# The start of a four-layer transformer kernel: x by column halves, its last row blocks turned inside the first weight chunk, and two multiplications of a zeroed tile ahead of them

## The reference

```python
def rms_norm(x, g):
    xf = x.astype(jnp.float32)
    y = xf * lax.rsqrt(jnp.mean(xf * xf, axis=-1, keepdims=True) + NORM_EPS)
    return (y * g.astype(jnp.float32)).astype(x.dtype)
...
h = rms_norm(x, ln1[l])
u = h @ w_in          # 256x1024 times 1024x(about 8000), the first of many such products
```

## Time and profile before

| what | value |
|---|---|
| median of 3 runs | 2510.94 us (2510.31 to 2512.36) |
| span of the profiled execution | 2510.4 us |
| TensorE busy in the span | 2489.0 us (99%) |
| VectorE, ScalarE, GpSimd busy | 1809.0, 1519.6, 154.1 us |
| first transpose of x starts | 6.71 us |
| first multiplication of chunk 0 starts | 10.53 us |
| first multiplication of the narrow product starts | 16.29 us |

### The profile page before, as it was taken

One profiled execution on the slowest core, in us unless ns is written; L12 is line 12 of the kernel. 1 busy time (PEld: TensorE's weight loads), 2 busy tenths in 40 slices (PEclk: granted clock), 3 DMA queues, 4 the chain that ended last, 5 costly groups with the idle time before them and its releaser, 6 DMA issues.

```text
span 2510.4 us, 31997 instructions
## 1 busy us (share of the span) xinstructions
PE 2489.0 (99%) x11868; PEld 2053.5 (82%) x11868; DVE 1809.0 (72%) x1809; ACT 1519.6 (61%) x1581; POOL 154.1 (6%) x133
## 2 busy tenths in 40 slices
PE   8999999999999999999999999999999999999998
PEld 7888888888888888888888887888888888888877
DVE  6587655657775554765555577988989888898888
ACT  6565544555554454545445556777777777777776
POOL 0101000010020000110000023000000000000010
PEclk9999999999999999999999999999999999999999
DMA  6444555444455564555554456999999999999996
GB/s 260 151 159 167 178 186 188 172 160 151 159 177 188 190 207 151 182 181 176 194 185 155 164 193 235 380 370 383 380 382 384 375 384 375 386 373 386 368 406 253
DMA packets 90683, 633.75 MB, mean 252 GB/s; under 512 B 10462, under 2 KB 10838, under 8 KB 15841
## 3 DMA queue, kind: packets, MB, share of 16 engines
q1 hardware_dynamic: 85584, 616.63, 65.7%
q0 software_dynamic: 4720, 15.57, 1.8%
q10 hardware_dynamic: 288, 0.33, 0.0%
HBM read 625.00 MB, written 7.48 MB: 252 GB/s over the span
## 4 chain that ended last, share of the span: by engine, by line
PE 98%; DMA 1%; DVE 0%; issue 0%; ACT 0%; SPq 0%; ACTq 0%; DVEq 0%
PE bank L785 14%; PE bank L787 13%; PE bank L786 13%; PE bank L1360 8%; PE bank L1362 8%; PE bank L1361 8%; PE bank L1333 4%; PE bank L1335 4%; PE bank L1334 4%; PE bank L767 4%; PE bank L800 4%; PE bank L802 4%; PE bank L801 4%; PE bank L1181 1%; PE bank L1180 1%; PE bank L1179 1%
## 5 line engine op out<-in xcount | busy, mean ns | idle before, releaser
L1903 DVE TENSOR_TENSOR w_lo<-raw,w_hi 128x2048 fp32r<-128x2048 f32 x583 | 1342.7, 2305 | 416.7 <-ACT w_hi L1450 401.3
L1450 ACT ACTIVATE w_hi<-raw 128x2048 fp32r<-128x2048 f32 (+1 forms) x588 | 1120.4, 1907 | 264.5 <-PE bank L802 117.4
L785 PE MATMUL bank<-w_hi,xhi 128*128 128x512 f32 x1456 | 580.1, 398 | 0.8 <-DVE w_lo L1913 0.2
L787 PE MATMUL bank<-w_lo,xhi 128*128 128x512 f32 x1456 | 568.7, 391 | 0.0
L786 PE MATMUL bank<-w_hi,xlo 128*128 128x512 f32 x1456 | 568.0, 390 | 0.0
L1360 PE MATMUL bank<-w_hi,xhi 128*128 128x512 f32 x896 | 359.4, 401 | 0.6 <-DVE w_lo L1903 0.3
L1362 PE MATMUL bank<-w_lo,xhi 128*128 128x512 f32 x896 | 350.6, 391 | 0.0
L1361 PE MATMUL bank<-w_hi,xlo 128*128 128x512 f32 x896 | 350.0, 391 | 0.0
L785 PEld LDWEIGHTS bank<-w_hi,xhi 128*128 128x128 f32 x1456 | 273.9, 188 | 61.8 <-issue 4.1
L787 PEld LDWEIGHTS bank<-w_lo,xhi 128*128 128x128 f32 x1456 | 273.5, 188 | 58.3
L786 PEld LDWEIGHTS bank<-w_hi,xlo 128*128 128x128 f32 x1456 | 274.1, 188 | 53.1
(11 more groups left out here) (377 smaller groups left out, 2384.2 us busy)
## 6 DMA issues: line engine op xcount, KB each, us to landing
raw<-in_wexpert SPq DMA_DIRECT2D x336, 1024.0 KB, 5.0
raw<-in_wdense SPq DMA_DIRECT2D x248, 1024.0 KB, 4.7
expert_rows<-y POOLq DMA_DIRECT2D x7, 512.0 KB, 4.8
expert_rows<-back POOLq DMA_DIRECT2D x3, 512.0 KB, 3.9
x<-in_x SPq DMA_DIRECT2D x2, 512.0 KB, 4.5
raw<-in_wdense SPq DMA_DIRECT2D x4, 256.0 KB, 5.9
biasT<-bias_rows POOLq DMA_DIRECT2D x1, 1024.0 KB, 7.1
normal_rows<-hnorm POOLq DMA_DIRECT2D x1, 1024.0 KB, 8.1
```

The lines of the kernel that those rows point to most:

```text
L785: mm(bank[banks[t]][:, :], xhi[:, k0 + k, tok], wh, start=start and k == 0, stop=False)
L787: last = mm(bank[banks[t]][:, :], xhi[:, k0 + k, tok], wl, start=False, stop=stop and k == 3)
L1450: return nc.scalar.activation(dst, src, f, **kw)
L1903: V.tensor_tensor(lo[:, c % RAW, :], raw[:, c % RAW, :], hi[:, c % HI, :].bitcast(F32), ALU.subtract).then_inc(lo_ready, 1)
```

## The change

Three things are done, all in the first microseconds.

1. x comes as two column halves (512 columns of all 256 rows, 512 KB each) in place of two row tiles. The first half has a semaphore of its own, `x_first`. In SyncE's order the first half stands first, then pieces 0 and 1 of chunk 0, then the second half, then pieces 2 and 3; the rest follows as before.
2. TensorE turns only groups 0 and 1 ahead of chunk 0. Groups 2 and 3 are turned in the middle of chunk 0, ahead of its third column block.
3. VectorE first fills 512 columns of `gates` with zeros, and TensorE multiplies this tile with itself twice (float32, 128x512, into bank 7) before it waits for x.

```diff
+            def fetch_piece(i):
+                w = slice(512 * i, 512 * i + 512)
+                sp.dma_start(raw[:, 0, w], a["wdense"][0][:, w]).then_inc(first_in[i] if i < 3 else raw_full[0], 16)
+            def fetch_columns(o, arrived):
+                sp.dma_start(x[:, :, o:o + 512], a["x"][0][:, o:o + 512].rearrange("(t p) d -> p t d", p=P)).then_inc(arrived, 16)
             def fetch_first():
-                for i in range(4):
-                    w = slice(512 * i, 512 * i + 512)
-                    sp.dma_start(raw[:, 0, w], a["wdense"][0][:, w]).then_inc(first_in[i] if i < 3 else raw_full[0], 16)
+                fetch_columns(0, x_first)
+                fetch_piece(0)
+                fetch_piece(1)
+                fetch_columns(512, x_loaded)
+                for i in (2, 3):
+                    fetch_piece(i)
...
-            for t in range(NT):
-                sp.dma_start(x[:, t, :], a["x"][0, t * P:t * P + P, :]).then_inc(x_loaded, 16)
...
                     if ready is None:
-                        pe.wait_ge(x_loaded, 16 * NT)
+                        pe.wait_ge(x_first if i < 2 else x_loaded, 16)
...
                 pe.wait_ge(free[X[1]], ev(key, X[1]))
-                if READY[key] is not None:
-                    norm(key, (2, 3))
+                norm(key, (2, 3))
...
+            pe.wait_ge(warm_set, 1)
+            for i in range(WARM):          # WARM = 2
+                mm(bank[X[3]][:, :], gates[:, 0, 0:P], gates[:, 0, 0:512], start=True, stop=True)
             pe.wait_ge(ident_loaded, 16)
...
-                    if ready is None or k[2] == "moe":
+                    if ready is None:
+                        norm(k, (0, 1))
+                    elif k[2] == "moe":
                         norm(k, range(4))
...
+            V.memset(gates[:, 0, 0:512], 0.0).then_inc(warm_set, 1)
```

More of the change, by code:

```diff
@@ L426, in program @@
         up_done = sem("branch_half_done")
+        warm_set, x_first = sem("warm_tile_set"), sem("x_first_columns_in")
         x_loaded, cst_loaded, par_loaded = sem("x_loaded"), sem("cst_loaded"), sem("par_loaded")
@@ L1482, in squares @@
                     if n == 0:
-                        act.wait_ge(x_loaded, 16 * NT)
+                        act.wait_ge(x_first, 16)
+                        act.wait_ge(x_loaded, 16)
                     for b, v in ready or []:
@@ L2710, in load @@
                 pool.dma_start(dst, src).then_inc(par2_loaded, 16)
-            pool.wait_ge(x_loaded, 16 * NT)
+            pool.wait_ge(x_first, 16)
+            pool.wait_ge(x_loaded, 16)
             pool.dma_start(onehot[:, :], a["onehot"]).then_inc(bias_loaded, 16)
@@ L2858 @@
 NNARROW = 2
+WARM = 2
 NPAR2 = L1 + 2
```

## The result

| | median | runs | span of the profiled execution |
|---|---|---|---|
| before | 2512.34 us (2510.31 to 2514.26) | 20 | 2510.4 us |
| changed | 2517.06 us (2515.17 to 2518.41) | 20 | 2512.8 us |

The ratio is 1.0018, with a 95% interval of 1.0012 to 1.0025: slower by 4.7 us (3.0 to 6.3). The forecast was 2510.9 in 2509.8 to 2512.7, so the time lies outside the range, and the side is wrong. A second timing gave 2515.46 against 2512.21: 1.0012 (1.0003 to 1.0021), slower by 3.3 us.

A forecast was written before the change was run, and what follows sets the result against it. TensorE, busy 2489.0 of 2510.4 us, was taken as the bound; the earlier start of chunk 0 would become a wait for the constants, so 0 (quick) to +0.3 us (slow), taken as 0: 2510.9 us, range 2509.8 to 2512.7.

The forecast's parts named there:

- Whether ScalarE and VectorE keep up: ScalarE and VectorE after the inner transposes: `w_hi` of chunk 1 starts 0.3 to 1.5 us later, all hidden.
- Behind that ScalarE waits for others again: After `w_lo` of chunk 2, ready at 25.7 to 26.9 us, ScalarE was taken to wait for other engines again.
- quick end: Upper clock level: chunk 0 from 8.6 to 14.9 us, chunk 1's `w_hi` 0.3 us later, sum 0.
- slow end: Lower clock level for transposes: chunk 0 from 9.3 to 16.6 us, chunk 1's `w_hi` 1.5 us later, sum +0.3.
- B: Rival: TensorE's clock at the lower level in chunk 0 after an idle gap; +0.5 to +2.6 us, middle 2512.3; chance 0.25.
- room ahead of the constants: 1.2 us at the end of chunk 0 that a slow stretch could use up before TensorE loses time.
- the row on which my forecast rests: Narrow product's first weight load at 16.26 us, after 0.38 us idle, read as TensorE waiting for constants landing at 16.07.
- x by halves: Start of the kernel: first half of x lands 3.8 us after issue, first transpose about 5.3 us, 1.4 us earlier.
- They can't come earlier: Constants: same bytes ahead of them in as many issues, so TensorE is released at 16.26 us as now.
- My own line on `par`: If `par` came no earlier, ScalarE's first copy would start at 7.0 us and chunk 0 at 9.6.
- The zeros: Two products of zeros ahead of x take 2.1 to 4.1 us, ending between 3.2 and 5.8 us.

The follow-up runs named there:

- e7: The kernel before with two extra 128x1024 copies on ScalarE ahead of the rounding of chunk 1: 2514.24 against 2512.49 us, ratio 1.0006.
- e3: The changed kernel with two more multiplications of zeros in TensorE's idle gap ahead of chunk 0: 2514.74 against 2512.49 us, ratio 1.0008.
- e5: The kernel before with only the memset and the two multiplications of zeros added: 2512.77 against 2512.62 us, ratio 1.0001.
- e1: The changed kernel with all 16 transposes ahead of chunk 0 again, zeros and column halves kept: 2514.49 against 2512.49 us, ratio 1.0005.
- e6: The kernel before with only x as two column halves, no zeros, all transposes ahead of chunk 0: 2514.08 against 2512.62 us, ratio 1.0006.
- e9: The changed kernel with ScalarE's two squares of x moved into its wait ahead of group 2: 2515.10 against 2512.00 us, ratio 1.0009.
- e10: The changed kernel with two more multiplications of zeros in TensorE's gap and ScalarE's squares in its wait for group 2: 2512.88 against 2512.21 us, ratio 1.0002.
- e4: The kernel before with only groups 2 and 3 turned inside chunk 0, no zeros or column halves: 2516.69 against 2512.62 us, ratio 1.0016.
- again4: The changed kernel as it is, profiled once more: the product at 44 us came 3.46 us late.
- again3: The changed kernel as it is, profiled once more: the product at 44 us came 3.57 us late, span 2513.3 us.

## Why the prediction was wrong

**The step that failed** is "Whether ScalarE and VectorE keep up", and in it the sentence "Behind that ScalarE waits for others again". I followed ScalarE only up to `w_lo` of chunk 2, found it just in time, and closed the book. But the series goes on to the product at 44 us, and before the change TensorE already waited there. There was no room at all: e7 shows that a delay of ScalarE's rounding from 13.59 to 15.56 passes in full, +1.97 us there and +1.95 at the product. My own quick end (+0.3) and slow end (+1.5) for that rounding were thus the sum, not a side condition. With the clock up they hold: e3 has +1.17, between the two.

**The rival that came true** is B, with 0.25. Its price was put at +0.5 to +2.6, middle 2512.3. Its mechanism is in the rows above: an idle time of 2.06 us (I said 2.0 to 2.4), then the lower level in chunk 0. What was mis-sized is the room. I had it eat 1.2 us of room ahead of the constants and priced the chain behind group 2 at "about 0.3 more". In fact the rounding came 2.5 to 3.6 us late and all of it counted. The 3.5 us "later" for ScalarE's work, which stand in my own text, were nearly what the profiles show; I put only a tenth of them into the price. I had also taken B as the less likely of the two. It was there in all seven profiles of the changed kernel, whether the clock rose early or not: about eight or more of the first twelve multiplications were slow in each.

**The constants.** I called the row at 16.26 "the row on which my forecast rests". The wait is real: e5 has 0.41 us idle ahead of the narrow product, though chunk 0 started 0.4 us earlier there. But it is no cap on a loss, only on a gain, and the loss came by another engine. In the changed kernel chunk 0 ended at 17.9 and the wait didn't count. Nor was its time right: I had TensorE released at 16.26 as before, and it is 17.0. In e3, where the clock stays up and TensorE gets there first, the constants are issued at 6.24 in place of 5.47 and land 10.6 us later, at 16.84:

```profile
6.24 0.43 SPq L737 DMA_DIRECT2D cst<-in_cst  x1
17.02 0.27 PE L920 MATMUL bank<-xhi,wsm_hi 128*28 128x256 f32 x1 [0.84 <-issue]
```

So the wait swallows the whole head start and 0.7 us more.

**x by halves.** First transposes at 6.02 in the profile (5.6 to 6.1 in the other six), forecast 5.3. The first half took 5.0 us from issue to landing, not 3.8. I had expected the small transfers to gain by the rule on turns between queues (the Trainium skill, DMA: Bandwidth & Descriptors, Queues, rings and completion order). The traces agree only in part. The identity took 2.7 to 4.4 us in the thirteen profiles with x by halves, and less than 4.0 in eleven of them, against 4.0 to 4.2 in the six with x by row tiles; `par` took 5.2 to 6.1 against 5.5 to 5.8. What all thirteen show is the first half of x held up: 4.5 to 5.1 us, against 3.8 to 4.0 for a row tile. Whether the turns between the queues do it, the half-long runs alone or the pieces that stand right behind, no run here tells. DMA issues of the changed kernel (KB, us to landing), against the earlier trace rows:

```profile
x<-in_x SPq DMA_DIRECT2D x1, 512.0 KB, 5.0
ident_t<-in_ident ACTq DMA_DIRECT2D x1, 64.0 KB, 3.0
par<-in_par ACTq DMA_DIRECT2D x1, 256.0 KB, 5.6
x<-in_x SPq DMA_DIRECT2D x1, 512.0 KB, 7.1
cst<-in_cst SPq DMA_DIRECT2D x1, 794.5 KB, 10.8
```

"They can't come earlier" was right for what stands behind x, but they can come later, a cost that I had at nothing: chunk 1 landed 0.7 to 1.0 us later in e1 and e6, and the constants, issued at 6.00 here, at 16.8 in place of 16.07. Chunk 0 started at 9.3 to 10.3 in the seven profiles, against 8.6 to 9.3 forecast. My own line on `par` had it at 9.6, and the range left that out; in e9 and e10 ScalarE's first copy does wait for `par`. And GpSimd's DMAs, which wait for the second half, started 3.3 us later (10.20 in place of 6.91), not 1.5; nothing on the chain waited for them.

**The zeros.** Duration as worked out: 3.78 us, forecast up to 4.1. Transposes at the upper level in some profiles (8 in 1.06 us), at the lower in others (1.94). Neither trace nor median shows that they do anything for the time (e5).

**Transposes and the clock.** The rule that transposes don't count as busy (the Trainium skill, TensorE: Matmul & The Clock Gate, Part 4) would give rival B for another reason. In e7, whose start is the kernel before's, the clock was up by the second multiplication after 3.65 us of transposes alone. e4 has the same start with only eight of the sixteen transposes and 1.88 us of idle time behind them, and there the first nine multiplications are slow. So the rows stand against the rule, and the loss came from the gap that the moved transposes left, not from their kind.

**The range.** It ended at 2512.7, only 0.4 us above the median that the kernel before had in twenty runs (2512.34; the three shown had 2510.94). Of the 6.2 us between forecast and measured time, 1.4 come from that and 4.7 from the change.

## What to carry to other kernels

Follow a delayed engine to the first place where the bounding engine already waits for it, however small that wait is; an idle time of 0.4 us in front of one product says that the chain behind it has no room. Work that seems to fill idle time can be what keeps TensorE's clock up, and other engines may be waiting for its results: before moving it, ask for both. And a stretch of 25 us may have two bounds, one on TensorE and one beside it, which take turns.

## What the hardware showed that was not expected

- The level of the clock at the start differs from execution to execution of one kernel. With the same program on TensorE it rose at 4.5 to 7.5 us and fell at 7.9 to 10.9, and in one profile (again4) it didn't rise before 13.9. The low stretch was 3.4 or 6.8 us long.
- An idle time of 2.06 us amid dense work was followed by a fall; 1.43 us (e5), 0.97 us (e3) and 0.18 us (e10) were not. The length of the gap doesn't decide alone: in again3 TensorE was idle from 6.65, and the granted clock fell at 7.95, after 1.3 us.
- The granted clock is given as 1.00 at the start of an execution while multiplications take twice their time: e4's row for 10.60 to 14.70 has 1.00 with 10 multiplications in 4.06 us. There the pace is what tells the level, not the column.

```profile
10.60:14.70 4.10, 4.06 (x10) 1.00 1.00 358
```

- Behind 44 us all kernels take nearly the same: the span less the start of the product is 2464.5 to 2467.1 us in all nineteen profiles, with no order by kernel (2465.9 before, 2465.2 to 2466.3 in the seven of the changed kernel). There is an order by the clock at the router. The low stretch there was 3.4 us long in two profiles (2464.5 and 2464.8), 6.8 us in twelve (2465.0 to 2466.3) and 10.2 us in five (2466.5 to 2467.1). That is an order, not a shown cause: no run was made to change it.
